# Weight tiles that begin at different multiples of 16 bytes in SBUF

## What is computed

```python
# first block
h = rmsnorm(x);  proj = h @ w_in                    # 1024 x 5128: q, k, v, f, g_b, g_c, hc, two gates
ya = g_b * causal_conv(g_c * hc)                    # 512 channels
yb = forgetting_attention(q, k, v, logf)            # 8 heads of 64
merged = sigmoid(gate_conv) * (ya @ w_branch[0]) + sigmoid(gate_attn) * (yb @ w_branch[1])
x = x + rmsnorm(merged @ w_out)
h = rmsnorm(x);  g, u = split(h @ w_gate_up)        # 1024 x 5632
x = x + rmsnorm((silu(g) * u) @ w_down)             # 2816 x 1024
# second block: differential attention with ALiBi, 16 heads
h = rms_norm(x);  q, k, v, z = split(h @ l0_w_in_2) # 1024 x 8192
o = head_norm(softmax(q1 k1) @ v - lam * softmax(q2 k2) @ v) * silu(z)
x = x + o @ l0_w_out_2                              # 2048 x 1024
```

## Time and profile before

| | before |
|---|---|
| median of 2 executions | 1270.14 us (1269.72 to 1270.57) |
| the profiled execution | 1270.14 us |
| its span (first to last instruction) | 1268.4 us |
| TensorE matmul busy | 1262.2 us, 100% |
| TensorE weight load busy | 1073.3 us, 85% |
| VectorE, ScalarE, GpSimd busy | 804.6, 604.7, 283.7 us |
| granted TensorE clock | 1.00 |

### The profile page before, as it was taken

The page is one execution under the profiler, slowest core; times in us unless marked ns, Lnnn a source line. Parts: engine busy times, 40 slices in busy tenths (PEclk is TensorE's granted clock), DMA queues, the critical chain, the costliest instruction groups (busy, mean ns, idle before and its releaser), DMA issues.

```text
span 1268.4 us, 18237 instructions
## 1 busy us (share of the span) xinstructions
PE 1262.2 (100%) x7106; PEld 1073.3 (85%) x7106; DVE 804.6 (63%) x1594; ACT 604.7 (48%) x1268; POOL 283.7 (22%) x188
## 2 busy tenths in 40 slices
PE   9999999999999999999999999999999999999999
PEld 7788888888889999999888888888888888888787
DVE  5435664333479889887333647676767677677744
ACT  4436655223444544545233445556555555556630
POOL 2022310000046656650001412021212112020000
PEclk9999999999999999999999999999999999999999
DMA  6322232333441443343236322322223322224611
GB/s 238 108 59 75 59 100 67 100 100 100 153 179 61 140 133 100 101 134 116 78 104 216 117 67 68 100 84 84 88 89 92 107 94 84 84 84 129 226 56 75
DMA packets 106408, 134.79 MB, mean 106 GB/s; under 512 B 9681, under 2 KB 73425, under 8 KB 106322
## 3 DMA queue, kind: packets, MB, share of 16 engines
q1 hardware_dynamic: 96146, 112.39, 28.0%
q10 hardware_dynamic: 10176, 21.24, 4.7%
HBM read 123.91 MB, written 9.70 MB: 105 GB/s over the span
## 4 chain that ended last, share of the span: by engine, by line
PE 97%; DVE 2%; issue 0%; ACT 0%; DMA 0%; POOL 0%; DVEq 0%
PE ps L953 14%; PE ps L955 14%; PE ps L954 14%; PE ps L958 9%; PE ps L960 9%; PE ps L959 9%; PE ps L1188 5%; PE ps L1191 5%; PE ps L1190 5%; PE ps L1252 3%; PE ps L1262 1%; PE ps L1234 1%; PE ps L1286 1%; DVE wlo L1650 1%; PE ps L1276 1%; PE ps L1277 1%
## 5 line engine op out<-in xcount | busy, mean ns | idle before, releaser
L1650 DVE TENSOR_TENSOR wlo<-raw,whi 128x512 fp32r<-128x512 f32 (+1 forms) x294 | 235.0, 826 | 179.2 <-ACT whi L1315 178.3
L1315 ACT ACTIVATE whi<-raw 128x512 fp32r<-128x512 f32 (+2 forms) x338 | 208.6, 649 | 114.6 <-PE ps L955 73.3
L953 PE MATMUL ps<-whi,hth 128*128 128x512 f32 x464 | 189.4, 408 | 0.0
L955 PE MATMUL ps<-wlo,hth 128*128 128x512 f32 x464 | 181.4, 391 | 0.0
L954 PE MATMUL ps<-whi,htl 128*128 128x512 f32 x464 | 181.3, 391 | 0.0
L958 PE MATMUL ps<-hth,whi 128*128 128x512 f32 (+1 forms) x416 | 164.4, 395 | 0.0
L960 PE MATMUL ps<-hth,wlo 128*128 128x512 f32 (+1 forms) x416 | 159.0, 382 | 0.0
L959 PE MATMUL ps<-htl,whi 128*128 128x512 f32 (+1 forms) x416 | 158.9, 382 | 0.0
L2106 POOL TENSOR_TENSOR wlo<-raw,whi 128x384 fp32r<-128x384 f32 (+1 forms) x44 | 49.1, 1132 | 415.2 <-ACT whi L1315 415.2
L953 PEld LDWEIGHTS ps<-whi,hth 128*128 128x128 f32 x464 | 87.3, 188 | 20.9 <-issue 3.4
L955 PEld LDWEIGHTS ps<-wlo,hth 128*128 128x128 f32 x464 | 87.1, 188 | 19.2
(11 more groups left out here) (360 smaller groups left out, 2901.1 us busy)
## 6 DMA issues: line engine op xcount, KB each, us to landing
raw<-in_w_gate_up SPq DMA_DIRECT2D x44, 512.0 KB, 4.8
raw<-in_l_w_in SPq DMA_DIRECT2D x32, 512.0 KB, 4.3
raw<-in_l_w_in SPq DMA_DIRECT2D x16, 1024.0 KB, 5.2
raw<-in_w_in SPq DMA_DIRECT2D x13, 1024.0 KB, 5.1
raw<-in_w_down SPq DMA_DIRECT2D x10, 1024.0 KB, 4.9
raw<-in_l_w_out SPq DMA_DIRECT2D x8, 1024.0 KB, 5.1
raw<-in_w_in SPq DMA_DIRECT2D x26, 256.0 KB, 3.4
raw<-in_w_branch SPq DMA_DIRECT2D x8, 512.0 KB, 3.8
```

The source lines that it names most:

```text
L953: e.matmul(o, ah, wh[:, cs], start=a, stop=False)
L955: m = e.matmul(o, ah, wl[:, cs], start=False, stop=z)
L1315: return e.activation(out, in_, ACT.Copy, **how)
L1650: return e.tensor_tensor(out, src, hi_part.bitcast(F32), ALU.subtract)
```

## The change

Each tile gets an offset of `4 * (5 * n % 16)` columns, that is (5n mod 16) times 16 bytes: 0 to 240 bytes. The second place moves from column 2048 to 2176, so that the longest offset fits. The Strassen ring (`slot_of`), the special tiles and everything else are as they were. The steps, their order, their number, their shapes and their waits are the same.

```diff
         for n, h in enumerate(self.h):
+            h.offset = 4 * (5 * n % 16)
             if h.pre is None:
                 h.pre = [n + 1]
@@
         wlo_all = sbuf(ctx, "wlo", [P, 4096 + 256], F32R)
-        whi, wlo = ([t[:, 2048 - 2048 * i:4096 - 2048 * i] for i in range(2)] for t in (whi_all, wlo_all))
@@
         def wide(n):
             h = H[n]
-            return special[h.special] if h.special else (whi[h.slot][:, :], wlo[h.slot][:, :])
+            if h.special:
+                return special[h.special]
+            o = 2176 * (1 - h.slot) + h.offset
+            return whi_all[:, o:o + 2048], wlo_all[:, o:o + 2048]
```

## The result

The changed kernel takes 1284.07 us (median of 1283.97 and 1284.17) against 1270.14 us before: a ratio of 1.0111, with a 95% interval of 1.0095 to 1.0127. It is 14 us slower. The forecast was 1267.6 us, range 1256 to 1275; the time lies outside the range, on the other side.

The account below looks back on a forecast made before the run. TensorE, through the distance between matmul starts, was taken to bound the kernel. Gains of 0.8 + 0 + 1.7 + 0 = 2.5 us off 1270.14 us gave 1267.6 us, range 1256 to 1275.

Parts of the forecast that it names:

- What bounds the kernel: Whole kernel: TensorE is busy 1262.2 of 1268.4 us, so only the distance between matmul starts matters.
- The collision in the earlier trace: `gu` against Strassen step, 256 columns: weight load and moving operand beginning alike within 256 bytes cost 6.7 ns a matmul.
- (b): The 3540 matmuls with 512 columns in steady flow: no change, 0 us.
- (c): 512-column matmuls right behind transposes or scores: part of their extra 5.0 ns goes, 1.7 us gained.
- The first: Rival: steady-flow 512-column matmuls collide too, so new starts gain at least 22.8 us there, 1246.5 us in all; chance 0.09.
- the new starts cost: Rival: 512-column matmuls slow down at the new offsets, at 231.7 ns each 17.7 us more, 1288 us; chance 0.08.
- (a): 120 matmuls with 256 moving columns, tiles 31 and 106: each falls from 120.0 to 113.3 ns, 0.8 us gained.
- (d): Weight-tile splits on ScalarE and VectorE: any slowdown from the offsets lies beside matmuls, so cost nothing.

Follow-up runs that it names:

- e4_gap: Kernel before, second place at 2176, with 64 bytes left free ahead of hth, so activations and everything behind begin 64 bytes later: 1292.17 us, ratio 1.0166.
- e8_shift64: Kernel before with the Strassen ring's shift at 256 bytes in place of 320: 1280.11 us, ratio 1.0072.
- e5_gap_all64: Against the kernel before, everything from hth on, all weight tiles and the Strassen ring begin 64 bytes later; second place at 2176: 1270.12 us, ratio 0.9999.
- p1_sweep: Separate program, TensorE alone on zeros, operand starts varied in 16-byte steps from 0 to 240: 226.7 to 234.6 ns with 512 columns and 128 stationary.
- e6_moving: Changed kernel with its offsets kept only for moving weight tiles, 0 for stationary ones: 1278.31, 1278.81, 1285.58 and 1287.42 us, ratio 1.0098.

## Why the prediction was wrong, step by step

**What bounds the kernel** was right: nothing but TensorE's distances moved.

**The collision in the earlier trace rows** was right in what it saw; e4_gap and e8_shift64 bring it about and e5_gap_all64 takes it away again, for 10 us. But of the other fifteen starts of the stationary operand in p1_sweep only 64 and 192 bytes reach 113.3 ns; the rest take 116.7 to 120.0 ns. The Trainium skill's rule of two independent read ports that never wait ("SBUF — State Buffer", section Who interferes with whom) would make the changed kernel as fast as before; 233.3 against 226.7 ns with TensorE alone disagrees.

**The step that failed is (b)**, and in it the inference from the earlier trace rows: "with 512 columns there is room beside the 106.7 ns ... the load may collide and nobody waits for it". It took 226.7 ns for the stream's own rate, 17/16 of the columns, on one width (and 113.3 ns for 256). Widths in between show a loss of fixed size instead, and the present starts already carry it. The prediction named this as its rival (two numbers only, 226.7 - 120.0 = 256 columns at 2.4 GHz) and then discarded it with a row whose stationary operand has 16 columns. That row's premise was that a short load leaves no loss; p1_sweep shows that with 16 columns the loss is there and depends on the start by 9 ns. The weights `wf2` begin at 224, 32, 96 and 160 bytes, so the moving operand stands 32, 224, 160 and 96 bytes on from them. For these p1_sweep's last column has 226.7, 231.1, 230.1 and 231.1 ns, in the mean 229.8 (an estimate, if only the difference counts), near the row's 229.3; equal starts would have had 231.1. The row spoke of 16 stationary columns and could decide nothing for 128. What the runs showed in place of the 0 of (b) and the 1.7 us of (c) is a cost of 13.4 us: 11.4 in steady flow, 2.0 in the first eight matmuls behind transposes and the like.

**The rivals.** The first had the mechanism (equal starts cost 13.3 ns with 512 columns too) and the wrong sign: it took for granted that another start loses less, since the one example with 256 columns did. The second, "the new starts cost", is what happened. Its price was 5.0 ns on 3540 matmuls, 17.7 us; measured were 3.7 ns on 2196 and 3.9 ns on 1344, 13.4 us. It had a chance of 0.08, on the ground that one stationary operand off the grid costs little; for a moving one the prediction itself said that no row speaks. The range then ended at 1275, ahead of that rival's own 1288.

**(a)** Mis-sized: tile 31 at 176 bytes runs at 118.3 ns, not 113.3. Its special neighbour 30, whose addresses didn't change, is no clean control: it went from 119.8 to 119.0 ns in the mean, as if it went on in the flow that it finds. The step in the changed kernel:

```profile
378.37 0.28 PE L961 MATMUL ps<-hth,whi 128*128 128x256 f32 x1
...
379.79 0.28 PE L961 MATMUL ps<-hth,yah 128*128 128x256 f32 x1
```

Twelve in 1.42 us. The gain of (a) was 0.2 us in place of 0.8.

**(c)** Wrong: the loss behind transposes doesn't go with other starts. In the first eight matmuls behind them the distance grew by 1.6 ns where the weights move and by 1.9 where they are stationary. At equal starts the loss dies away to 226.7 ns; at others the flow mostly stays at the like of it.

**(d)** Right: 621 and 688 ns for the two splits, as before, and TensorE's waits are 2.8 and 0.8 us with two of 0.4 and 0.2 more.

## What stays open

Why the two reads lose time to each other is not shown, only on what it depends. That it is the two reads that meet is itself argued, from how the distance depends on both starts. The exact use of an offset below 64 bytes (both at 80 cost 3.3 ns) was not followed further. Of 51 executions of the kernel before in the runs beside these experiments 12 took 1276 to 1277.5 us in place of 1270. That they do so by the Strassen step's second flow fits in size: had the flow of 117.8 ns gone on behind the wait at 410.2 us, some 1540 matmuls would have taken 4.5 ns more each, an estimated 6.9 us. It is not shown: none of the twelve was profiled, only e6_moving.

## What to carry to other kernels

Where TensorE bounds a kernel of fp32r matmuls, read the distance from start to start in an undisturbed stretch and compare it with the columns at the granted clock: here 13.3 ns of 226.7 are not columns. Begin both operands of 512-column matmuls with 128 stationary columns at multiples of 256 bytes, and with 256 columns set one of them 64 bytes apart; spreading the starts over all multiples of 16 bytes, as if to avoid a clash, cost 1.1% of the whole here. And a rate read at one width is no rate: a second width that doesn't divide evenly, here 384, would have told 17/16 from a fixed loss before anything was forecast.

## What the runs showed of the hardware that was not expected

How the operands begin within 256 bytes sets the pace of fp32r matmuls with 128 stationary columns, in p1_sweep 226.7 to 234.6 ns with 512 columns and 113.3 to 120.0 with 256, with all other engines silent; the start that is best for the one width is not for the other. bf16 matmuls don't show it (215 to 216 ns). And a deterministic program can settle into either of two flows at the same addresses, 113.3 or 117.8 ns a matmul, and then keeps it for up to 190 us, or changes it at a wait of half a microsecond; it makes 7 us of 1280.
